# Sample-state products in stacked half precision, and chunk states ahead of the exponent differences

## The reference

```python
b = jnp.cumsum(log_f, axis=1)
scores = jnp.einsum('bthk,btshk,bshk->bhts', q, decay, k)
o = jnp.einsum('bhts,bshv->bthv', scores, v) + jnp.einsum('bthk,bhkv->bthv', q * jnp.exp(b), s0)
s_new = jnp.exp(b_last)[..., None] * s0 + jnp.einsum('bshk,bshv->bhkv', k * jnp.exp(b_last[:, None] - b), v)
```

## Time and profile before

| what | value |
|---|---|
| median of 3 runs | 1739.92 us (1738.65 to 1740.34) |
| profiled execution, its own time | 1742.57 us |
| its span | 1741.0 us |
| TensorE matmul busy | 1567.8 us (90%) |
| VectorE busy | 904.5 us (52%) |
| ScalarE busy | 654.0 us (38%) |
| GpSimd busy | 154.3 us (9%) |
| mean granted TensorE clock | 0.931 of full |

### The profile page before, as it was taken

One profiled execution on the slowest core, in us unless ns is written; L12 is line 12 of the kernel. 1 busy time (PEld: TensorE's weight loads), 2 busy tenths in 40 slices (PEclk: granted clock), 3 DMA queues, 4 the chain that ended last, 5 costly groups with the idle time before them and its releaser, 6 DMA issues.

```text
span 1741.0 us, 31399 instructions
## 1 busy us (share of the span) xinstructions
PE 1567.8 (90%) x12107; PEld 1251.0 (72%) x12107; DVE 904.5 (52%) x1389; ACT 654.0 (38%) x920; POOL 154.3 (9%) x126
## 2 busy tenths in 40 slices
PE   4699999989699999999867999999886999999994
PEld 3477777767578888788755777777765888887883
DVE  4766644444565555533266665444356555553334
ACT  3645523332353334422155452333225443333213
POOL 2111111100200000000030111000002000000002
PEclk8799989988899999999978899999888999999997
DMA  6132222221123332233221224232031223322321
GB/s 192 46 90 77 75 75 75 74 74 55 57 73 97 96 96 77 70 93 95 82 66 51 74 74 111 57 88 78 27 97 48 88 83 96 96 81 74 97 66 51
DMA packets 175035, 138.05 MB, mean 79 GB/s; under 512 B 5064, under 2 KB 169192, under 8 KB 174776
## 3 DMA queue, kind: packets, MB, share of 16 engines
q1 hardware_dynamic: 168192, 113.46, 22.0%
q0 software_dynamic: 5408, 18.60, 3.8%
q10 hardware_dynamic: 1372, 5.16, 0.9%
HBM read 125.12 MB, written 12.07 MB: 79 GB/s over the span
## 4 chain that ended last, share of the span: by engine, by line
PE 77%; DVE 9%; ACT 6%; issue 4%; DVEq 2%; ACTq 1%; DMA 1%; SPq 0%
PE ACC L510 61%; PE SCR L624 2%; PE OT L632 2%; PE SCR L662 1%; ACT WH L830 1%; DVE X L1193 1%; PE OT L684 1%; PE SCR L545 1%; PE SCR L727 1%; DVE Z L1222 1%; DVE Fb L1206 1%; DVE WL L1153 1%; PE OT L600 1%; DVEq L1261 1%; PE OT L599 1%
## 5 line engine op out<-in xcount | busy, mean ns | idle before, releaser
L510 PE MATMUL ACC<-XH,WH 128*128 128x280 f16 x2432 | 502.6, 289 | 70.8 <-DVE XL L1196 43.1
L510 PE MATMUL ACC<-XL,WH 128*128 128x280 f16 x2432 | 502.4, 289 | 0.0
L510 PE MATMUL ACC<-XH,WL 128*128 128x280 f16 x2432 | 501.6, 289 | 0.0
L510 PEld LDWEIGHTS ACC<-XH,WH 128*128 128x128 f16 x2432 | 238.7, 101 | 153.0 <-DVE XL L1196 45.6
L1153 DVE SCALAR_TENSOR_TENSOR WL<-stage,WH 128x2048 f16<-128x2048 f32 (+1 forms) x116 | 245.9, 2120 | 182.0 <-ACT WH L830 170.2
L510 PEld LDWEIGHTS ACC<-XL,WH 128*128 128x128 f16 x2432 | 243.3, 100 | 58.6
L510 PEld LDWEIGHTS ACC<-XH,WL 128*128 128x128 f16 x2432 | 243.3, 100 | 58.0
L830 ACT ACTIVATE WH<-stage 128x2048 f16<-128x2048 f32 (+1 forms) x116 | 204.8, 1766 | 103.7 <-PE ACC L510 86.9
L510 PE MATMUL ACC<-shared,WH 128*128 128x280 f16 x1408 | 225.2, 283 | 0.2
L510 PEld LDWEIGHTS ACC<-shared,WH 128*128 128x128 f16 x1408 | 137.6, 98 | 30.8 <-issue 0.8
L510 PE MATMUL ACC<-shared,WL 128*128 128x280 f16 x704 | 141.5, 283 | 0.0
(11 more groups left out here) (238 smaller groups left out, 1791.4 us busy)
## 6 DMA issues: line engine op xcount, KB each, us to landing
stage<-in_w_in_dram SPq DMA_DIRECT2D x64, 512.0 KB, 5.3
stage<-in_w_a_dram SPq DMA_DIRECT2D x44, 512.0 KB, 4.3
stage<-in_w_b_dram SPq DMA_DIRECT2D x44, 512.0 KB, 4.8
stage<-in_w_down_dram SPq DMA_DIRECT2D x32, 384.0 KB, 3.3
stage<-in_w_down_dram SPq DMA_DIRECT2D x32, 320.0 KB, 3.7
out_dram<-shared POOLq DMA_DIRECT2D x16, 512.0 KB, 3.9
stage<-in_w_o_dram SPq DMA_DIRECT2D x16, 512.0 KB, 3.9
shared<-in_state_hgrn_dram POOLq DMA_DIRECT2D x8, 512.0 KB, 5.7
```

The lines of the kernel that those rows point to most:

```text
L510: last = mm(ACC[:, acc, h, 0:HALF], lhs, x[:, xk + k, h * HALF:(h + 1) * HALF], start=begin, stop=end)
```

## The change

Two parts.

The first concerns the sample-state products. The keys and the values of the 32 sample tokens are split into a high half-precision part and a low one (the rest that the high part misses), and stacked three times on the partitions: 96 rows hold keys as high, high, low and values as high, low, high. One half-precision pass over 96 rows then gives high x high + high x low + low x high. For this KE and V carry the sample columns three times (a copy on VectorE for KE, a second read out of the accumulator on ScalarE for V), the transposes take 96 columns, ScalarE writes all 96 rows of `KV3` in half precision and a float32 copy `VTS` of the values for `sample_output`, and VectorE then overwrites the two low blocks with the rest, transpose less high part (`low_sample_rows`); the tables `seq` and `k_dec_s` repeat their rows. `VX` has 96 rows in half precision and waits for `kv_low` instead of `tok_ready`, and the scratch bank of the transposes is released by VectorE instead of ScalarE. In an HGRN group `low_sample_rows` stands on VectorE behind the gate's first operation, in group 4 ahead of the key's rotation, in retention steps behind the copy of the first score job.

The second part: in HGRN groups the chunk states `b()` stand ahead of `hg_exponents` on VectorE.

```diff
-        VX = sb("VX", [TS, DEC_BATCH, P])
-        KVTS = sb("KVTS", [TS, 2, P])
+        VX = sb("VX", [TS3, DEC_BATCH, P], F16)
+        KV3 = sb("KV3", [TS3, 2, P], F16)
+        VTS = sb("VTS", [TS, P])
...
-                pool.wait_ge(tok_ready, hh + 1)
-                nc.gpsimd.tensor_tensor(VX[:, :, :], KVTS[:, 1:2, :].to_broadcast([TS, DEC_BATCH, P]), bcast(seqm[0:TS, :], P),
+                pool.wait_ge(kv_low, hh + 1)
+                nc.gpsimd.tensor_tensor(VX[:, :, :], KV3[:, 1:2, :].to_broadcast([TS3, DEC_BATCH, P]), bcast(seqm[0:TS3, :], P),
                                         ALU.mult).then_inc(vx_ready, 1)
...
-                            last = nc.tensor.transpose(SCR[0:TS, bank, i * P:(i + 1) * P], src[:, TP:T], ident)
+                            last = nc.tensor.transpose(SCR[0:TS3, bank, i * P:(i + 1) * P], src[:, TP:TP + TS3], ident)
...
-                mm(SCR[:, bank, :], KVTS[:, 0, :], VX[:, 4 * n:4 * n + 4, :].rearrange("p b v -> p (b v)"),
+                mm(SCR[:, bank, :], KV3[:, 0, :], VX[:, 4 * n:4 * n + 4, :].rearrange("p b v -> p (b v)"),
                    start=True, stop=True).then_inc(scr_full, 1)
...
-                mm(cols_, KVTS[:, 1, :], PTSS[:, :], start=True, stop=False, skip_group_check=True)
+                mm(cols_, VTS[:, :], PTSS[:, :], start=True, stop=False, skip_group_check=True)
...
-                f(halves(buf[:, 0:T]), ACC[:, c, :, 0:HALF], ACT.Copy, scale=INV_W).then_inc(acc_read[c], 1)
+                last = f(halves(buf[:, 0:T]), ACC[:, c, :, 0:HALF], ACT.Copy, scale=INV_W)
+                if buf is V:
+                    last = f(twice(V), ACC[:, c, 1:2, HALF - TS:HALF].to_broadcast([P, 2, TS]), ACT.Copy, scale=INV_W)
+                last.then_inc(acc_read[c], 1)
...
-                f(KVTS[:, :, :], SCR[0:TS, 0, 0:2 * P].rearrange("p (n v) -> p n v", n=2), ACT.Copy).then_inc(scr_read[0], 1)
+                f(KV3[:, :, :], SCR[0:TS3, 0, 0:2 * P].rearrange("p (n v) -> p n v", n=2), ACT.Copy)
+                f(VTS[:, :], SCR[0:TS, 0, P:2 * P], ACT.Copy).then_inc(kv_high, 1)
                 act.drain().then_inc(tok_ready, 1)
...
-                f(KVTS[:, 0, :], SCR[0:TS, 0, 2 * P:3 * P], ACT.Copy, scale=tab[0:TS, ds(cols["k_dec_s"][0] + p, 1)])
-                f(KVTS[:, 1, :], SCR[0:TS, 0, 3 * P:4 * P], ACT.Copy).then_inc(scr_read[0], 1)
+                f(KV3[:, 0, :], SCR[0:TS3, 0, 2 * P:3 * P], ACT.Copy, scale=tab[0:TS3, ds(cols["k_dec_s"][0] + p, 1)])
+                f(KV3[:, 1, :], SCR[0:TS3, 0, 3 * P:4 * P], ACT.Copy)
+                f(VTS[:, :], SCR[0:TS, 0, 3 * P:4 * P], ACT.Copy).then_inc(kv_high, 1)
                 act.drain().then_inc(tok_ready, 1)
...
+            def low_sample_rows(hh, at, decay):
+
+                keys, values = (slice(2 * TS, TS3), KV3[2 * TS:TS3, 0, :]), (slice(TS, 2 * TS), KV3[TS:2 * TS, 1, :])
+                dve.wait_ge(kv_high, hh + 1)
+                if decay is None:
+                    tt(keys[1], SCR[keys[0], 0, at:at + P], keys[1], ALU.subtract)
+                else:
+                    stt(out=keys[1], in0=SCR[keys[0], 0, at:at + P], scalar=tab[keys[0], ds(cols["k_dec_s"][0] + decay, 1)],
+                        in1=keys[1], op0=ALU.mult, op1=ALU.subtract)
+                tt(values[1], SCR[values[0], 0, at + P:at + 2 * P], values[1], ALU.subtract).then_inc(scr_read[0], 1)
+                dve.drain().then_inc(kv_low, 1)
...
                 dve.drain().then_inc(f_ready, 1)
+                if low_rows is not None:
+                    low_rows()
...
+                nc.vector.tensor_copy(twice(KE), KE[:, TP:T].unsqueeze(1).to_broadcast([P, 2, TS]))
                 dve.drain().then_inc(ew_ready, 1)
...
                 for job in RT_JOBS:
+                    if job is RT_JOBS[1]:
+                        low_sample_rows(hh, 2 * P, p)
...
+                hgrn_rows = (lambda: low_sample_rows(hh - 1, 0, None)) if steps else None
                 if kind == 0:
-                    hg_gate(l, head, tile)
-                    hg_exponents(l, head)
+                    hg_gate(l, head, tile, hgrn_rows)
                     if b is not None:
                         b()
+                    hg_exponents(l, head)
                     if d is not None:
                         out_gate(hh - 1)
                     hg_query(l, head, j + 1, mixed, steps)
                 else:
                     if after_hgrn:
 
+                        hgrn_rows()
                         dve.wait_ge(tok_ready, hh)
```

More of the change, by code:

```diff
@@ L46 @@
 T = TP + TS
+TS3 = 3 * TS
 HALF = T // 2
@@ L143, in const_tables @@
     put("mask32", causal)
-    put("seq", tok[:, None] // DEC_SEQ == np.arange(DEC_BATCH)[None, :])
+    put("seq", np.tile(tok[:, None] // DEC_SEQ == np.arange(DEC_BATCH)[None, :], (3, 1)))
     log_g = np.log1p(-np.exp2(-5.0 - np.arange(HEADS)))
@@ L154, in const_tables @@
     put("k_dec", np.where(left >= 0, np.exp(np.maximum(left, 0) * log_g[None, None, :]), 0.0) * root)
-    put("k_dec_s", np.exp((DEC_SEQ - 1 - tok % DEC_SEQ)[:, None] * log_g[None, :]) * root)
+    put("k_dec_s", np.tile(np.exp((DEC_SEQ - 1 - tok % DEC_SEQ)[:, None] * log_g[None, :]) * root, (3, 1)))
     put("gamma4", np.broadcast_to(np.exp(DEC_SEQ * log_g), (P, HEADS)))
@@ L218, in hybrid_decoder_step @@
         Fb, T1, T2, T3, B, Q, QS, QD, KE, E, V, G = (
-            sb(n, [P, T + 2]) for n in ("Fb", "T1", "T2", "T3", "B", "Q", "QS", "QD", "KE", "E", "V", "G"))
+            sb(n, [P, T + (2 * TS if n in ("KE", "V") else 2)]) for n in ("Fb", "T1", "T2", "T3", "B", "Q", "QS", "QD", "KE", "E", "V", "G"))
         at = [0]
@@ L291, in hybrid_decoder_step @@
         tok_ready, vx_ready, pts_ready, states_ready = sem("tok_ready"), sem("vx_ready"), sem("pts_ready"), sem("states_ready")
+        kv_high, kv_low = sem("kv_high"), sem("kv_low")
         decays_used = sem("decays_used")
@@ L328, in bcast, with twice @@
             return ap.unsqueeze(2).to_broadcast([ap.shape[0], ap.shape[1], n])
+        def twice(t):
+            return t[:, T:T + 2 * TS].rearrange("p (a t) -> p a t", a=2)
         def level_halves(n, src=None):
@@ L653, in rest_transposes @@
                         nc.tensor.transpose(SCR[0:TAIL, 0, n * P:(n + 1) * P], src[:, 4 * P:TP], ident)
-                        last = nc.tensor.transpose(SCR[0:TS, 0, (2 + n) * P:(3 + n) * P], src[:, TP:T], ident)
+                        last = nc.tensor.transpose(SCR[0:TS3, 0, (2 + n) * P:(3 + n) * P], src[:, TP:TP + TS3], ident)
                     last.then_inc(scr_full, 1)
@@ L1196, in norm_apply, with hg_gate @@
                         tt(XL[:, m - 2, :], X[:, m - 2, :], XH[:, m - 2, :], ALU.subtract).then_inc(x_ready, 1)
-            def hg_gate(l, p, tile):
+            def low_sample_rows(hh, at, decay):
[8 more added lines that the diff above has]
+                dve.drain().then_inc(kv_low, 1)
+            def hg_gate(l, p, tile, low_rows=None):
                 n = l * HEADS + p
```

## The result

The changed kernel takes 1760.61 us (median of 4 runs, 1759.22 to 1764.23), the kernel before, run beside it, 1740.13 us: 1.0121 times as long, 95% interval 1.0104 to 1.0139. Slower was forecast, but 6.5 us, not 20.5, and the time lies above the range. The profiled executions compare 1757.7 us with 1741.0, 16.7 more: the one of the kernel before took 2.4 us more than its median, the one of the changed kernel 1.4 less.

A forecast was written before the change was run, and what follows sets the result against it. Bound: stall, sample products and half clock, with slot 24 also waiting for ScalarE's Q read. Terms 10.4 - 1.8 - 4.2 - 1.0 + 0.6 + 2.5 = +6.5 on 1739.92 gave 1746.4 us, range 1724 to 1757.

The forecast's parts named there:

- I take 2.2 lost (0 to 3.1): HGRN groups, behind slot 24: half clock after the moved wait loses 2.2 us, less 0.2, so +2.0 a group.
- Second and third groups: HGRN groups with steps, second and third of each layer: each ends 2.8 us later, +11.2 for four.
- The first groups: First HGRN group of each layer: +1.4 us in layer one, -2.2 in layer two, whose earlier half speed need not recur.
- Group 4: Retention head 0 with the last HGRN head's steps, two groups: shorter products give -0.9 us each, -1.8 in all.
- the retention groups: Six retention groups: shorter products save 1.5 us, the later scratch bank costs 0.8; each gains 0.7, -4.2 in all.
- the projection with what follows it: Output projection, two of them: products save 1.3 us, bank wait costs 0.8; each gains 0.5, -1.0 in all.
- +2.5: Four retention groups: 0.8 more waiting may make the clock fall; a quarter of 10 us taken, +2.5.
- The 0.8 wait before the second score job: Retention stages: VTS copy and VectorE's two operations free scratch bank 0 later, so the second score job waits 0.8 us.
- The port did not go to VectorE: Rival: VectorE not held by GpSimd, scan ends 1.2 us earlier instead of 0.7 later; about 1735 us, chance 0.17.
- The clock did not stay up: Rival: the moved wait at slot 24 costs 0.8 us but brings no half-speed stretch; about 1731 us, chance 0.06.
- The Q read was in the way: Rival that it is not: stall of 17.7 us and 30 us of products go; about 1699 us, chance 0.08.
- Worse than forecast: Rival: half speed for 6 us after each moved wait and in every retention group; past 1757 us, chance 0.06.

The follow-up runs named there:

- the products alone: Changed kernel with VectorE's order put back (exponent differences first, states behind), half-precision products kept: 1729.79 us, ratio 0.9949 against the kernel before.
- with the outputs behind: Changed kernel with the last four chunk outputs and sample outputs of HGRN steps put off to slots 28 and 29, mean squares to 31: 1755.17 us, ratio 1.0105.

## Why the prediction was right in sign and wrong in size

- **The mechanism held.** Products 0.23 us apart (0.22 forecast); the stall in front of them not gone but moved to slot 24, for ScalarE's Q read, six times, 5.55 us in the second group (5.7 forecast). The Q read came 3.9 us later against the copy (3.7), and the experiments part it: 3.0 for the states (3.0), 0.8 for the low rows and the held L1206 (0.7). Slot 24 opened 1.0 later against the copy (0.8).
- **The step that failed** is the sentence "I take 2.2 lost (0 to 3.1)" for the half-speed stretch behind slot 24. With the 0.2 taken off it forecast 2.0 more from slot 24 to the group's last stretch; the trace shows 6.15 (14.05 less 7.90). That is 4 us in each of the four steady groups, and the size came from the earlier trace rows, a retention wait with other work behind it. A nearer row was there: in the earlier trace rows the outputs behind slot 24, at half speed in layer two, took 3.6 us more, above the bound of 3.1. The runs show what should have stood there: where the clock falls within 1.5 us before slot 24 opens, the outputs and the 4-column sample outputs behind it run at half speed to the end, 13.7 us in all, which costs 6.15; with projection of 280 columns in their place it is 6.8 us at most. Second and third groups took 7.1 and 6.9 more from VX to VX, in place of 2.8.
- **The first groups** were to give +1.4 and -2.2; they gave +3.5 and +0.1. The half stretch there is 6.8 us, for the clock fell earlier, and a second one of 3.4 stands behind the sample outputs. The low clock that layer two had before was not saved, as the step assumed, but came again.
- **Group 4 and the retention groups** were better than forecast. Group 4: -1.4 each (-0.9). From VX to VX, four of six retention groups gave -0.5 (-0.7), and the projection with what follows it -1.2 each (-0.5). The other two gave -2.1 and -2.2: in the kernel before both began inside a half stretch (343.9 to 347.3 and 1146.1 to 1149.5), and the changed kernel has none there. That this is the cause was read from the clock alone, not tested; behind the sample outputs of retention heads there is still half speed, three stretches before and four after. So the "+2.5" for more half speed there had the wrong sign, some -3.3 (2.1 and 2.2 less 0.5 each). The 0.8 wait before the second score job came as forecast: 7.2 in 8. A bare sum over stages hides that two terms were wrong in opposite directions.
- **The rivals.** The port did not go to VectorE: L1232 was ready at 146.82, while VX ran to 147.18, and GpSimd's next instruction still went first; L1232 ended at 149.65, 0.6 after it, and took 2.83. The clock did not stay up. The Q read was in the way. "Worse than forecast" came true for the HGRN half of its condition and got 0.06; since nothing in the rows bounded the half stretch at 3.1 us lost and the earlier trace rows showed 3.6, it deserved more, and the range should have reached it.

## What to carry to other kernels

Moving work ahead of a chain delays all that the chain feeds: follow each delayed read to the accumulator or scratch bank it frees, and to whoever waits for that. A stall that is taken away before a product is only gained if the next wait lies far behind; here the products alone brought nothing inside the groups of layer one, and filling the wait with independent projection brought 0.9% (0.9942 to 0.9854). Price the half clock behind a new wait from a stretch with the same work behind it, and take the longest that the traces show as the bound: the same wait and the same outputs gave 6.8 us in one group and 13.7 in the next.

## What was not expected of the hardware

- TensorE's clock fell without idle time: behind 1.88 us of 4-column sample outputs, at 124.6, with the engine busy in every window around, and, when the sample outputs stood ahead of the wait, during them, at 156.1, 3 us after an idle stretch of 0.8.
- Waits of 4.2, 5.55 and 5.85 us were followed by half stretches of 13.7, 13.7 and 6.8 us; 5.55 us with projection behind it by 6.8, and 5.93 us with the outputs behind it, where the clock fell earlier, by 6.8. Idle time does not give the length. The sample outputs do not bring the clock down each time: with the outputs behind, the sample outputs at 175 ran at full speed in the second group, and the clock fell behind them in the third. What decides between these was not tried.
- The port pair of VectorE and GpSimd stayed with GpSimd over two instructions in a row. The Trainium skill, SBUF — State Buffer, "Who interferes with whom", says that the pair is an exclusive lock and that the order of issue decides who is blocked. The lock agrees with L1232, which took 2.83 us and ended 0.6 after the second of the two; but L1232 (146.82) waited before L430 began (147.15) and yet came after it, which the rule read by starting times does not give.
